# Neighbourhood attention on 256 keys a query block, with a narrower key-row projection and a reordered prologue

## What is computed

```python
def neighbourhood_attn(q, k, v, rpb):           # 8 heads of 64, rows = 8, window 8 rows x 16 columns
    col_start = jnp.clip(col - NA_WIN_W // 2, 0, GRID_W - NA_WIN_W)
    col_in = (col[None, :] >= col_start[:, None]) & (col[None, :] < col_start[:, None] + NA_WIN_W)
    def row_block(r):                            # every row sees all 8 rows
        s = jnp.einsum('bchd,bjkhd->bhcjk', q_r, k_r)
        s = jnp.where(col_in, s + bias, -jnp.inf)      # bias by row and column distance
        p = softmax(s over the 8 x 64 keys)
        return jnp.einsum('bhcjk,bjkhd->bchd', p, v_r)
```

## Time and profile before

| | us |
|---|---|
| median of 3 runs | 1574.56 (1573.95 to 1577.68) |
| the profiled execution, own time | 1573.36 |
| its span, first to last instruction | 1571.5 |
| mean granted TensorE clock | 0.993 |

### The profile page before, as it was taken

How to read it: one execution, slowest core, us unless ns; L and a number is a source line. 1 busy time by engine, 2 the same in 40 slices (tenths; PEclk the granted TensorE clock), 3 DMA queues, 4 the chain that set the end, 5 groups by cost and what they waited for, 6 DMA issues and landing times.

```text
span 1571.5 us, 19448 instructions
## 1 busy us (share of the span) xinstructions
PE 1519.6 (97%) x7408; PEld 1150.0 (73%) x7408; DVE 874.1 (56%) x1533; ACT 700.5 (45%) x1166; POOL 371.5 (24%) x435
## 2 busy tenths in 40 slices
PE   8899999999999999999999999999999999999996
PEld 5667665668777787877887887566877778787785
DVE  4523245665788436885343344565578843678532
ACT  3223436653533444553544344665453344455333
POOL 0011123432010003675210002343201000366310
PEclk9999999999999999999999999999999999999998
DMA  9478842123322341115234443211242234120421
GB/s 373 153 222 264 268 158 85 44 61 94 133 95 81 109 146 41 47 35 216 93 96 152 134 116 99 84 56 50 94 136 92 80 121 135 41 55 27 175 94 67
DMA packets 68124, 181.63 MB, mean 116 GB/s; under 512 B 20528, under 2 KB 20912, under 8 KB 65728
## 3 DMA queue, kind: packets, MB, share of 16 engines
q1 hardware_dynamic: 68032, 180.39, 35.6%
HBM read 155.69 MB, written 24.67 MB: 115 GB/s over the span
## 4 chain that ended last, share of the span: by engine, by line
PE 81%; DVE 8%; ACT 4%; DMA 3%; issue 2%; POOL 1%; SPq 0%; DVEq 0%; ACTq 0%; POOLq 0%
PE ps L494 20%; PE ps L495 20%; PE ps L496 20%; PE ps L1057 4%; PE ps L1008 3%; PE ps L1040 2%; PE ps L1025 2%; PE ps L302 2%; PE ps L1509 1%; PE ps L1492 1%; DMA at<-w_ada 1%; DVE w_lo L476 1%; PE ps L1543 1%; PE ps L1332 1%; DMA at<-z_kept 1%
## 5 line engine op out<-in xcount | busy, mean ns | idle before, releaser
L476 DVE TENSOR_TENSOR w_lo<-at,w_hi 128x1024 fp32r<-128x1024 f32 x162 | 201.3, 1243 | 375.7 <-ACT w_hi L468 375.6
L468 ACT ACTIVATE w_hi<-at 128x1024 fp32r<-128x1024 f32 x162 | 170.4, 1053 | 121.0 <-PE ps L496 121.0
L494 PE MATMUL ps<-h_e_hi,w_hi 128*128 128x512 f32 x480 | 191.1, 398 | 7.8 <-DVE w_lo L476 7.8
L496 PE MATMUL ps<-h_e_hi,w_lo 128*128 128x512 f32 x480 | 187.3, 390 | 0.0
L495 PE MATMUL ps<-h_e_lo,w_hi 128*128 128x512 f32 x480 | 187.2, 390 | 0.0
L494 PE MATMUL ps<-h_a_hi,w_hi 128*128 128x512 f32 x400 | 160.4, 401 | 3.6 <-DVE h_a_lo L526 3.0
L495 PE MATMUL ps<-h_a_lo,w_hi 128*128 128x512 f32 x400 | 157.0, 392 | 0.0
L496 PE MATMUL ps<-h_a_hi,w_lo 128*128 128x512 f32 x400 | 156.8, 392 | 0.0
L1165 POOL TENSOR_SCALAR at<-at,at 128x512 f32<-128x512 f32 x128 | 92.1, 732 | 129.7 <-DVE at L1118 129.7
L494 PEld LDWEIGHTS ps<-h_e_hi,w_hi 128*128 128x128 f32 x480 | 90.1, 188 | 43.6 <-DVE at L1318 11.7
L496 PEld LDWEIGHTS ps<-h_e_hi,w_lo 128*128 128x128 f32 x480 | 90.2, 188 | 19.2
(11 more groups left out here) (281 smaller groups left out, 3045.6 us busy)
## 6 DMA issues: line engine op xcount, KB each, us to landing
at<-blocks_in SPq DMA_DIRECT2D x162, 512.0 KB, 3.8
at<-w_ada SPq DMA_DIRECT2D x32, 512.0 KB, 4.8
at<-w_ada SPq DMA_DIRECT2D x8, 1024.0 KB, 17.9
at<-xs SPq DMA_DIRECT2D x4, 2048.0 KB, 10.5
z_kept<-at SPq DMA_DIRECT2D x32, 256.0 KB, 2.1
at<-z_kept SPq DMA_DIRECT2D x32, 256.0 KB, 2.8
at<-t_masked SPq DMA_DIRECT2D x16, 448.0 KB, 3.6
sg_kept<-at SPq DMA_DIRECT2D x16, 256.0 KB, 4.5
```

What stands on the lines that cost most here:

```text
L468: act.activation(whi[:, n % PAIRS], wring[:, n % SLOTS], ACT.Copy).then_inc(sem("w_hi"), 1)
L476: dve.tensor_tensor(wlo[:, n % PAIRS], wring[:, n % SLOTS], whi[:, n % PAIRS].bitcast(F32), ALU.subtract)\
L494: pe.matmul(o, stationary[0], moving[0], start=first, stop=False)
L496: return pe.matmul(o, stationary[1], moving[0], start=False, stop=final)
```

## The change

A query block of the neighbourhood heads is now 16 columns by 8 rows, shifted by 8 columns, so that its window lies in two of four key blocks of 16 columns (blocks i and i + 1; the last query block holds the 8 columns at either edge and takes key blocks 0 and 3). A head has four tiles of 128 queries by 256 keys, and is one step instead of two: 24 steps in stage C for 32. Queries are written in block order at eviction, keys are read in place in runs of 16 columns, values are stored in block order, and the value products write their results back to column order in PSUM, for two of the four key blocks in two parts of 128 queries. The bias table of a head is 512 wide instead of 896, made of one gather and two POOL operations, and three are held for two. Gating follows by GATED.

The key-row block is split into 32 high and 32 low columns in one 64-column operand and takes 16 products (pe_project_narrow). A constant krsum adds high and low rows and gives permuted and plain rows in one product; VectorE multiplies both from PSUM, with POOL's L897 gone.

In the prologue fewer folds lie between the ada steps, folds 13 to 15 lie behind the turn, ScalarE keeps the last four between its h pieces, the first two weight splits move into VectorE's h pieces, and two w_ada pieces are loaded ahead of the first two weight blocks.

The core of the diff:

```diff
-    FOLD_BANK = 2
-    FOLDS = (4, 6, 8, 10, 12, 14, 16, 16)
+    FOLD_BANKS = (2, 3, 2, 3, 2, 3, 2, 3, 2, 3, 2, 3, 2, 3, 4, 6)
+    FOLDS = (4, 5, 6, 7, 8, 9, 11, 12)
+    F_LATE = FOLDS[-1]
...
-            if k == 6:
-                groups[0].stream_weights(sp, PAIRS - PAIRS - SLOTS)
             sp.dma_start(ada_w[k], ada_part(0, k, 0, 4)).then_inc(sem(f"p_w{k}"), 16)
+        groups[0].stream_weights(sp, -SLOTS)
...
+        fold(F_LATE)
         ada_turn(pe, 0)
+        for c in range(F_LATE + 1, IC):
+            fold(c)
...
-        groups[0].act_h(act, 0, 0, h_A)
+        for c in range(DC):
+            groups[0].act_h(act, 0, 0, h_A, which=(c,))
+            if 2 <= c < 2 + IC - F_LATE:
+                n = F_LATE + c - 2
+                act.wait_ge(sem("p_fold"), n + 1)
+                b = ps(FOLD_BANKS[n])
+                act.activation(Gt[:, n], b[:, 0:P], ACT.Copy).then_inc(sem("p_kept"), 1)
...
-        for c in range(IC):
-            if c == IC - 2:
-                for b in range(PAIRS):
-                    groups[0].dve_split(dve, b)
+        for c in range(F_LATE):
...
-        groups[0].dve_h(dve, 0, 0, h_A, xT)
+        groups[0].dve_h(dve, 0, 0, h_A, xT, splits={1: 0, 2: 1})
...
+    def query_cols(ap, i):
+        if i == TM - 1:
+            return by_col(ap).rearrange("p r (u c) -> p r u c", c=HALF_W)[:, :, 0:8:7]
+        return by_col(ap)[:, :, BLK_W * i + HALF_W:BLK_W * (i + 1) + HALF_W]
+    def key_cols(ap, i):
+        v = by_col(ap).rearrange("p r (v c) -> p v r c", c=BLK_W)
+        return v[:, 0:TM:TM - 1] if i == TM - 1 else v[:, i:i + 2]
...
+            cols = slice(0, ROPE if b == B_KR else P)
+            act.activation(whi[:, n % PAIRS, :, cols], wring[:, n % SLOTS, :, cols], ACT.Copy).then_inc(sem("w_hi"), 1)
...
+            if b == B_KR:
+                dve.tensor_tensor(whi[:, n % PAIRS, :, ROPE:2 * ROPE], wring[:, n % SLOTS, :, 0:ROPE],
+                                  whi[:, n % PAIRS, :, 0:ROPE].bitcast(F32), ALU.subtract).then_inc(sem("w_lo"), 1)
+                return
...
+        def pe_project_narrow(pe, b, out_ap, src):
+            wait_split(pe, b)
+            for k in range(DC):
+                for n in range(2):
+                    last = pe.matmul(out_ap[0:2 * ROPE], whi[:, pair_of(b), k, 0:2 * ROPE], src[n][:, k],
+                                     start=(k == 0 and n == 0), stop=(k == DC - 1 and n == 1))
+            last.then_inc(sem("blk_done"), 1)
...
-                    for rr in range(2):
-                        src = bass.AP(tensor=rpb_pad.tensor, offset=h * RPB_R * PADW + (1 - rr) * PADW,
-                                      ap=[[1, GRID_W], [PADW, BANDS], [1, GRID_W]])
-                        sp.dma_start(T2raw[64 * rr:64 * rr + 64, h % 2].rearrange("p (e k) -> p e k", k=GRID_W), src)\
-                            .then_inc(sem(f"t2_raw{h % 2}"), 16)
+                        sp.wait_ge(sem("t2_band"), at("t2_band", h - 1))
+                    src = bass.AP(tensor=rpb_pad.tensor, offset=h * BLK_W * RPB_R * 2 * BLK_W,
+                                  ap=[[2 * BLK_W, ROWS], [RPB_R * 2 * BLK_W, BLK_W], [1, T // 2]])
+                    sp.dma_start(T2raw[:, h % 2], src).then_inc(sem(f"t2_raw{h % 2}"), 16)
...
+                for o, v, mask in ((0, near, band), (T // 2, wrap, edge)):
+                    new = T2new[:, h % 2, o:o + T // 2].rearrange("p (b k c) -> p b k c", b=2, c=BLK_W)
+                    last = pool.tensor_tensor(new, v, mask, ALU.add)
+                last.then_inc(sem("t2_band"), 1)
...
-                        dve.scalar_tensor_tensor(naq[1][:, n], ps(b % 4), NA_D ** -0.5, naq[0][:, n].bitcast(F32),
-                                                 ALU.mult, ALU.subtract).then_inc(sem("naqk_lo"), 1)
+                        for lo, hi, scores in zip(query_pieces(naq[1][:, n]), query_pieces(naq[0][:, n].bitcast(F32)), source_pieces(ps(b % 4))):
+                            last = dve.scalar_tensor_tensor(lo, scores, NA_D ** -0.5, hi, ALU.mult, ALU.subtract)
+                        last.then_inc(sem("naqk_lo"), 1)
...
-                        act.activation(naq[0][:, n], ps(b % 4), ACT.Copy, scale=NA_D ** -0.5).then_inc(sem("naqk_hi"), 1)
+                        for hi, scores in zip(query_parts(naq[0][:, n]), query_sources(ps(b % 4))):
+                            last = act.activation(hi, scores, ACT.Copy, scale=NA_D ** -0.5)
+                        last.then_inc(sem("naqk_hi"), 1)
...
-            dve.tensor_tensor(t1[0:32, 2], b_bank(J_KR)[0:32], cst("sin", 32), ALU.mult).then_inc(sem("b_t1"), 1)
+            for n in range(2):
+                dve.wait_ge(sem(f"sg_out{n}"), at(f"sg_out{n}", 16 * (DC // 2)))
+            dve.tensor_tensor(t0[0:ROPE, 2], b_bank(J_KR)[ROPE:2 * ROPE], cst("cos")[ROPE:2 * ROPE], ALU.mult).then_inc(sem("b_kt"), 1)
+            dve.tensor_tensor(t1[0:ROPE, 2], b_bank(J_KR)[0:ROPE], cst("sin", ROPE), ALU.mult).then_inc(sem("b_t1"), 1)
             dve.wait_ge(sem("b_t1"), at("b_t1", 1))
-            dve.wait_ge(sem("b_t0"), at("b_t0", 1))
+            dve.wait_ge(sem("b_kt"), at("b_kt", 1))
...
-            pool.wait_ge(sem("b_full"), at("b_full", J_KR + 1))
             for n in range(2):
                 pool.wait_ge(sem(f"sg_out{n}"), at(f"sg_out{n}", 16 * (DC // 2)))
-            pool.tensor_tensor(t0[0:32, 2], kr[0:32, :], cst("cos", 32), ALU.mult).then_inc(sem("b_t0"), 1)
...
-                    last = pe.matmul(o[0:32], const[0:32, perm0:perm0 + 32], kr[0:32, :], start=True, stop=True)
+                    last = pe.matmul(o[0:2 * ROPE], cst("krsum", 2 * ROPE), kr[0:2 * ROPE], start=True, stop=True)
...
-        HALVES = 2 * HEADS * 2
+        HALVES = 2 * HEADS + HEADS
...
+        GATED = (8, 12, 16, 20, 22, 24, 26, 28)
...
-                if h >= 2:
-                    sp.wait_ge(sem("c_max"), at("c_max", MLA_END + 4 * ((h - 2) // 2) + 2 + h % 2 + 1))
-                sp.dma_start(T2[:, h % 2], t2_masked[h]).then_inc(sem(f"t2_in{h % 2}"), 16)
+                if h >= 3:
+                    sp.wait_ge(sem("c_max"), at("c_max", MLA_END + h - 2))
+                sp.dma_start(T2[:, h % 3], t2_masked[h]).then_inc(sem(f"t2_in{h % 3}"), 16)
...
-                for m in range(2):
-                    col = (2 * half + m) * P
+                for m in range(TM):
                     for s, (a, b) in enumerate(((0, 0), (0, 1), (1, 0))):
                         for e in range(2):
                             r = 64 * e
-                            last = pe.matmul(ps(s_bank(j + e) + m), naq[a][r:r + 64, n, col:col + P], nak[b][r:r + 64, n],
-                                             start=(s == 0), stop=(s == 2))
-                            if m == 1 and s == 2:
+                            o = ps(s_bank(j + e) + m // 2)[:, 2 * P * (m % 2):2 * P * (m % 2 + 1)]
+                            last = pe.matmul(o.rearrange("p (b r c) -> p b r c", b=2, c=BLK_W), naq[a][r:r + 64, n, m * P:(m + 1) * P],
+                                             key_cols(nak[b][r:r + 64, n], m), start=(s == 0), stop=(s == 2))
+                            if m == TM - 1 and s == 2:
                                 last.then_inc(sem("c_s"), 1)
+            NEAR = ((3, 0), (0, 0)), ((1, 1), (2, 0)), ((0, 1), (1, 0)), ((2, 1), (3, 1))
...
-                            last = pe.transpose(ps(4 + q)[:, col:col + P], Pt[:, j % 4, e, s * P:(s + 1) * P], ident)
+                            m, k = (e, s) if j < MLA_END else (NEAR[s][e][0] // 2, 2 * (NEAR[s][e][0] % 2) + NEAR[s][e][1])
+                            last = pe.transpose(ps(4 + q)[:, col:col + P], Pt[:, j % 4, m, k * P:(k + 1) * P], ident)
...
+            def near_values(j, n):
+                for s, v in enumerate((0, 2, 1, 3)):
+                    if s == 2:
+                        pe.wait_ge(sem("c_pd"), at("c_pd", j + 1))
+                    for e in range(2):
+                        o = ps(6 + n % 2)[64 * e:64 * e + 64]
+                        w = nav[:, v, (2 * n + e) % HEADS]
+                        if v % 3:
+                            parts = [(by_col(o)[:, :, BLK_W * v - HALF_W:BLK_W * v + 3 * HALF_W].rearrange("p r (i c) -> p i r c", c=BLK_W), 0, 2)]
+                        else:
+                            parts = [(query_cols(o, NEAR[s][k][0]), k, k + 1) for k in range(2)]
+                        for q, lo, hi in parts:
+                            last = pe.matmul(q, w, PT[(j - 1 + e) % 4][:, 2 * P * s + P * lo:2 * P * s + P * hi],
+                                             start=(s == 0 and lo == 0), stop=(s == TM - 1 and lo == 1))
...
-                if i >= 8 and i % 4 == 0:
-                    c = i // 4 - 2
-                    dve.wait_ge(sem("c_pv"), at("c_pv", 4 * c + 4))
+                if i in GATED:
+                    c = GATED.index(i)
+                    dve.wait_ge(sem("c_pv"), at("c_pv", i - LV))
...
-                        for e in range(2):
```

(22 more changed lines are left out.)

## The result

| | before | after |
|---|---|---|
| median | 1575.7 us (1574.0 to 1577.7, 4 runs) | 1520.0 us (1518.8 to 1520.7, 4 runs) |
| profiled execution | 1573.4 us (span 1571.5) | 1518.8 us (span 1517.0) |
| first neighbourhood scores to last values, first group | 58.82 us | 36.11 us |

The ratio is 0.9646 (95% interval 0.9632 to 0.9661), so 3.5% faster. The forecast was 1523.8 us, with 1512 to 1541 as the range; the difference of the medians is 55.7 us where 50.8 were worked out.

The account below looks back on a forecast made before the run. TensorE was taken to bound the kernel, with VectorE hand-overs in the neighbourhood period. Neighbourhood -44.6, key-row block -3.6, rotary stage -0.8, prologue -1.8 sum to -50.8 us: 1522.6 profiled, 1523.8 median; range 1512 to 1541.

Parts of the forecast that it names:

- The neighbourhood half: Attention stage, first neighbourhood scores to last values: 36.5 us against 58.8, so -22.3 a group, -44.6 in all.
- Rival 1: Neighbourhood scores and values: weight loads bind, 1.1 + 0.5 us more in each of eight periods, 1537 us; chance 0.17.
- Rival 2: Neighbourhood value products: PSUM writes in runs cost extra, 2.2 us more in each of eight, 1541 us; chance 0.10.
- Rival 3: VectorE and ScalarE: half-width operations save little, bias operations 0.5 us rather than 0.35, 1530 us; chance 0.10.
- Rival 5: Neighbourhood value products: strided writes priced per element, 6.4 us or more extra a step, slower than before; chance 0.03.
- rival 4: More is won: values 1.9 us, tail 1.5 shorter, prologue -3.5, key sum quick, 1515 us; chance 0.12.
- The period: Neighbourhood half: values 2.25, scores with hand-over 1.57, bias 1.50, copy 0.64, half turn 0.66, sum 6.62 us; first two 6.25.
- of eight only the neighbours overlap: Value products of a split key block: the two heads overlap only where adjacent, 0.64 us against 0.47 unsplit.
- The tail: Last neighbourhood scores' end to last values' end: 15.8 us against 13.9, the last-but-one turn waiting for VectorE's gate and low part.
- Rotary stage: Start of the stage behind the key-row block: VectorE makes both products from PSUM, 0.6 us each; -0.4 a group, -0.8 in all.
- the chain runs through: Rotary stage: the path goes through the last stored gate block, POOL's product (1.3 us) and VectorE's key sum (1.73).
- Prologue: Turn 3.5 us sooner, VectorE's h chain ends 56.55, clock held, projections end 58.7 against 60.5: -1.8 us; bounds -3.5, +1.

Follow-up runs that it names:

- Experiment 7: Changed kernel with VectorE's copy of the turned bank ahead of the fourth bias operation and ScalarE's first three exponentials released by the third: 1518.05 us.
- wide_values: Changed kernel with no value product split, 16 instructions of 256 columns for 24, results in wrong query columns: 1519.5 us, value link 1.88 us.
- heads_in_turn: Changed kernel with all products of one head before the other's, in scores and values, instead of alternating: 1535.4 us; values 3.24 us, scores 2.72.
- experiment 4: Also wide_keyrow: changed kernel with the key-row block again computed by 24 products on 128 weight columns: 1523.5 us, ratio to the kernel before 0.9672.
- experiment 5: Changed kernel with eight more small TensorE products behind the prologue's last fold, so that TensorE does not stand idle: 1521.8 us.
- experiment 11: Changed kernel with early key sum, VectorE's period copy earlier and both tail copies moved: 1514.04 us; the same plus eight extra prologue products: 1515.4 us.
- early_keysum: Changed kernel with the key's rotary products and sum no longer waiting for the last stored gate blocks, GpSimd's products later: 1518.0 us.

## Why the prediction was right, and where its terms were off

**The mechanism held.** No new bound came: TensorE and its hand-overs to VectorE set the period, ScalarE and GpSimd stayed under it. The neighbourhood half was forecast at 36.5 us a group and took 36.1. Experiment 7, which moves VectorE's copy and shortens each period by 0.4 us, shows that the chain ran there. Rivals 1, 2, 3 and 5 are out: scores take 1.65 us and not 2.6; a write in runs costs nothing; bias operations stand 0.345 us apart and not 0.5. Of rival 4 the first term came true: values at 1.94 where it had 1.9.

**The period was right by terms of opposite sign.** Scores with hand-over: 1.57 forecast, 1.73 measured. The pairs start 0.12 us apart as taken from rows 6, but the first takes 0.22, and VectorE starts 0.08 behind the last. The first two periods were therefore 6.40 and not 6.25. Values: 2.25 forecast, 1.94 measured. The failed step is "of eight only the neighbours overlap": wide_values puts the split at 0.06 us, and heads_in_turn shows that overlap is lost only when far more instructions of one head stand together. Bias 1.47 for 1.50, copy and half turn 1.31 for 1.30. The tail was 15.2 for 15.8: three value steps, each 0.3 shorter, take 0.9 off, and the turn that I had waiting for VectorE's gate and low part waited for ScalarE's copy instead. That the period came out at 6.45 for 6.62 is in part luck.

**Key-row block**: 1.82 forecast, 1.81 measured, 3.5 in the total by experiment 4.

**Rotary stage**: 0.4 a group forecast, nothing measured in either (77.06 for 76.96 us, 18.83 for 18.81). The prediction's own sum, 2.9 against 3.1, gave only 0.2; the 0.4 was a choice between its bounds. Two steps failed. One is the price: the products from PSUM take 0.71 us from start to start and not 0.6, so the pair replaces GpSimd's 1.39 us by 1.42, and the sum stays at 1.7. The other is "the chain runs through" the key sum, in the first group: as changed, TensorE's query product (L1011) ends at 220.3, together with the sum, so that a quicker sum gains nothing. It was so before: L927 starts 10.09 us behind the turn (225.25 and 215.16), as L1011 does now (219.26 and 209.17), and 1.05 later, at 226.30, the sum ended too. In the second group the sum does bind, by 0.56 us, and the step held there; but the three operations take as long as those that they replace.

**Prologue**: 1.8 forecast, 2.5 measured, and the working was wrong twice. It compared the end of both projections (58.7) with the release by the first (60.5); before, six products of the second block still followed from 60.28 on, so that like with like the end was 61.64, and its own steps gave 2.9. And it took the clock as held: it fell, and the products from 47.8 to 50.7 came 0.43 us apart or more, so that the end was 59.1 and not 58.7. Held, 0.5 more would have been there (experiments 5 and 11). The first error hid 1.1 us of gain, the second 0.4 of loss. VectorE did end at 56.4, as forecast at 56.55.

**Not in the sum**: 1.6 us of the projection stage, by fewer waits for adaptive weights in the first group. Eleven profiles put this stage at 148.0 to 149.2 us (wide_keyrow less its 1.8), the kernel before at 151.7. That the new tables' fewer transfers (54618 packets for 68124) free the queues is a possible cause; it was not tried alone. A rival is the new order and timing of the prologue: the eight extra products of experiment 5, with the same transfers, move this stage by 3.9 us. The cause stays open.

**Together**, 50.8 became 54.5 by the spans: neighbourhood 0.8 more than forecast, prologue 0.7, projection stage 1.6, the clock in the second group 1.1, rotary stage 0.9 less; 0.4 is spread over the rest. Of the 3.7 us above the forecast, 2.7 were in no term of it: that the number came so near is in part luck, and the total alone would not have shown where it was off.

## What to carry to other kernels

Cost a period as a chain of links from start to start, engine by engine, and check each link alone: here the sum was right to 3% while two links were off by 9 and 16% in opposite directions. An operation that one engine does for another in a chain must be priced from start to start with what runs beside it, and it only counts while nothing else arrives at the same moment. When a wait is removed in a tail, look for the other input of the same instruction: the first copy moved gained nothing until the second moved too.

## What the runs showed of the hardware beyond this

A VectorE sum of two operands in SBUF, 32 x 512 f32, took 0.68 us alone (early_keysum, 215.43) and 1.67 us beside GpSimd's products (218.59 as changed). VectorE's products from PSUM at the same time (L958, L959) kept their 0.68. The Trainium skill (SBUF — State Buffer, Terms) has VectorE and GpSimd arbitrate for one port pair that is held for a whole instruction, the other being blocked; the trace agrees: the sum lost 0.99 us, less than one GpSimd product of 1.27, and ended 0.55 us behind the second of them (219.71), which is about its own 0.68 alone.

TensorE's loads of 128 columns on two row groups kept up with products of 256 columns, a pair each 0.12 us, and 24 small value instructions took 0.06 us longer than 16 larger ones of the same columns.
